# Second block's first columns between the products back, two projections interleaved by pairs of weight pieces, and two steps moved in the attention's queues

## The reference

```python
u2 = modulate(rmsnorm(h, norm_ffn_g[l]), sh2, sc2)
h = h + g2[:, None, :] * hier_moe(u2, ...)          # 16 experts: hid @ w2, summed
return rmsnorm(h, norm_final_g)                     # first block's end
...
xn = rmsnorm_2(h, norm_gain[i]).astype(dt)          # second block's start
proj = xn @ w_in[i]
aq, ak, av, ag, bq, bf, bi, bg, gate_a, gate_b = jnp.split(proj, split_pts, axis=-1)
...
fpre = bf.astype(f32).reshape(b, s, HGRN_HEADS, HGRN_KDIM)
log_f = jax.nn.log_sigmoid(fpre) + jnp.log1p(lb * jnp.exp(jnp.minimum(-fpre, EXP_CLIP)))
kb = (1.0 - lb) * jax.nn.sigmoid(-fpre)
qb = jax.nn.silu(bq.astype(f32)).reshape(b, s, HGRN_HEADS, HGRN_KDIM)
```

## Time and profile before

| | |
|---|---|
| median of 3 runs | 745.0 us (744.92 to 745.93) |
| the profiled execution | 744.99 us, of which span 743.7 us |
| PE busy | 712.0 us (96%), 3766 products |
| DVE busy | 500.4 us (67%) |
| ACT busy | 380.3 us (51%) |
| chain that ended last, by engine | PE 80%, DVE 9%, ACT 4%, DMA 2%, POOL 2% |
| granted TensorE clock, mean | 0.999 |

### The profile page before, as it was taken

The page is one execution under the profiler, slowest core; times in us unless marked ns, Lnnn a source line. Parts: engine busy times, 40 slices in busy tenths (PEclk is TensorE's granted clock), DMA queues, the critical chain, the costliest instruction groups (busy, mean ns, idle before and its releaser), DMA issues.

```text
span 743.7 us, 9899 instructions
## 1 busy us (share of the span) xinstructions
PE 712.0 (96%) x3766; PEld 573.5 (77%) x3766; DVE 500.4 (67%) x738; ACT 380.3 (51%) x549; POOL 90.2 (12%) x71
## 2 busy tenths in 40 slices
PE   3899999999999999999999999989999999999997
PEld 0587666778788877888887777769888877788886
DVE  1364785345579774775668898887998675555854
ACT  1353433556444444654547777747624548644532
POOL 0252385340010000000000000011002500000000
PEclk9999999999999999999999999999999999999999
DMA  9999787757335950666579999955544575536541
GB/s 317 364 291 372 253 323 272 258 171 283 113 116 184 366 175 18 197 221 192 178 242 314 362 349 364 370 203 153 148 132 134 165 224 150 169 117 198 168 141 57
DMA packets 100670, 164.07 MB, mean 221 GB/s; under 512 B 10768, under 2 KB 45293, under 8 KB 100494
## 3 DMA queue, kind: packets, MB, share of 16 engines
q1 hardware_dynamic: 98718, 155.53, 62.9%
q0 software_dynamic: 1904, 7.90, 3.1%
HBM read 162.33 MB, written 1.08 MB: 220 GB/s over the span
## 4 chain that ended last, share of the span: by engine, by line
PE 80%; DVE 9%; ACT 4%; DMA 2%; POOL 2%; SPq 1%; issue 1%; ACTq 0%; DVEq 0%
PE p L574 22%; PE p L576 21%; PE p L575 21%; DVE s_rawr L1841 3%; PE p L643 3%; PE p L632 2%; PE p L1234 2%; ACT s_hi L1395 1%; PE p L702 1%; PE p L678 1%; DMA s_ZC<-in_w_ada_dram 1%; POOL s_BI L492 1%; ACT s_L L1445 1%; DMA s_raw<-in_w_exp_up_dram 1%; PE p L690 1%
## 5 line engine op out<-in xcount | busy, mean ns | idle before, releaser
L1841 DVE TENSOR_TENSOR s_rawr<-s_raw,s_hi 128x1024 fp32r<-128x1024 f32 x223 | 271.8, 1249 | 45.9 <-ACT s_hi L1395 45.3
L1395 ACT ACTIVATE s_hi<-s_raw 128x1024 fp32r<-128x1024 f32 x240 | 245.2, 1054 | 88.0 <-PE p L576 53.7
L574 PE MATMUL p<-s_hi,s_Ah 128*128 128x512 f32 (+1 forms) x464 | 186.5, 402 | 1.7 <-POOL s_rawr L473 1.0
L576 PE MATMUL p<-s_hi,s_Al 128*128 128x512 f32 (+1 forms) x464 | 179.8, 387 | 0.0
L575 PE MATMUL p<-s_rawr,s_Ah 128*128 128x512 f32 (+1 forms) x464 | 179.4, 387 | 0.0
L574 PEld LDWEIGHTS p<-s_hi,s_Ah 128*128 128x128 f32 x464 | 87.3, 188 | 27.0 <-issue 6.9
L576 PEld LDWEIGHTS p<-s_hi,s_Al 128*128 128x128 f32 x464 | 87.2, 188 | 18.4
L575 PEld LDWEIGHTS p<-s_rawr,s_Ah 128*128 128x128 f32 x464 | 87.4, 188 | 15.8 <-issue 0.2
L574 PE MATMUL p<-s_hi,s_Bh 128*128 128x512 f32 x192 | 76.3, 397 | 0.2 <-DVE s_rawr L1841 0.2
L576 PE MATMUL p<-s_hi,s_Bl 128*128 128x512 f32 x192 | 75.0, 391 | 0.0
L575 PE MATMUL p<-s_rawr,s_Bh 128*128 128x512 f32 x192 | 74.9, 390 | 0.0
(11 more groups left out here) (375 smaller groups left out, 857.2 us busy)
## 6 DMA issues: line engine op xcount, KB each, us to landing
s_raw<-in_w_in_dram SPq DMA_DIRECT2D x80, 512.0 KB, 4.0
s_GS<-in_w_ada_dram SPq DMA_DIRECT2D x16, 1024.0 KB, 7.6
s_raw<-in_w_exp_gate_dram SPq DMA_DIRECT2D x64, 256.0 KB, 4.1
s_raw<-in_w_exp_up_dram SPq DMA_DIRECT2D x64, 256.0 KB, 5.4
s_raw<-in_w_exp_down_dram SPq DMA_DIRECT2D x32, 512.0 KB, 5.7
s_raw<-in_w_gate_dram SPq DMA_DIRECT2D x16, 512.0 KB, 5.8
s_raw<-in_w_ret_out_dram SPq DMA_DIRECT2D x8, 512.0 KB, 3.5
s_raw<-in_w_o_dram SPq DMA_DIRECT2D x8, 512.0 KB, 8.4
```

Source lines behind the costliest of these rows:

```text
L574: pe.matmul(o, xh, wh, start=start, stop=False)
L576: return pe.matmul(o, xl, wh, start=False, stop=stop)
L1395: act.activation(T.hi[:, i % NHL, :], T.raw[:, i % NRAW, :], ACT.Copy).then_inc(*S.hi(i))
L1841: dve.tensor_tensor(T.lo[:, i % NRAW, :], T.raw[:, i % NRAW, :], T.hi[:, i % NHL, :].bitcast(F32), ALU.subtract).then_inc(*S.lo_dve(i))
```

## The change

It has five parts. (1) `silu(15)` and `hidden(15)` now stand after the high and low parts of dn14 and before those of dn15. (2) `u3_cols(0)` stands before `rows_back(2, 1)` and `u3_cols(2)` behind it; before, both stood behind it. (3) The pieces of bq and bf are loaded, converted and used in the order bq 0, bq 1, bf 0, bf 1, bq 2, bq 3, bf 2, bf 3, with `u3_cols(4)` in front of bf 0 and `u3_cols(6)` in front of bf 1. VectorE's queue is rewritten to match; ScalarE's stays as it was there, so its conversions now belong to other pieces. (4) The last piece of av is used between the transposes of aq and those of ak. (5) In ScalarE's queue of the attention two conversions move ahead of `exps(0)`, and the copy of the probabilities moves ahead of the silu of ag. No work is added or removed.

```diff
--- before.py
+++ after.py
@@ -88,7 +88,9 @@
             some(f"up{e}", range(4))
         if e:
             some(f"dn{e - 1}", range(2))
-    for name in SECOND:
+    for hs in ((0, 1), (2, 3)):
+        some("bq", hs), some("bf", hs)
+    for name in SECOND[2:]:
         some(name, range(4))
     for n in range(2):
         some(f"ub{n}", range(2)), some(f"ua{n}", range(2))
@@ -1172,6 +1174,11 @@
             q.wait_ge(*S.dve_rows.at("lo", 0, 1))
         down(n, 0, (0, 1), (f"dn{n}", 0, 1))
         down(n, 1, (0, 1), (f"dn{n}", 1, 1))
+
+    def u3_cols(k0):
+        q.wait_ge(*S.dve_moe.at("x3", min(k0 // 2, 2), 1))
+        turn(lambda tt, k: T.X3[:, tt, 128 * k:128 * k + 128], ("u3", k0), S.dve_cols.at("u3", k0))
+
     hidden_cols(15)
     q.wait_ge(*S.dve_rows.at("lo", 1, 1))
     rows_back(0, 0), rows_back(1, 0)
@@ -1180,28 +1187,26 @@
         down(15, 0, (c,), None)
         down(15, 1, (c,), ("dn15", c, 1))
     rows_back(2, 0)
-    rows_back(0, 1), rows_back(1, 1), rows_back(2, 1)
+    rows_back(0, 1), rows_back(1, 1)
+    t_free[0] = t_free[1] = S.dve_moe.at("lo", 15)
+    u3_cols(0)
+    rows_back(2, 1)
+    u3_cols(2)
     m_free[0] = m_free[1] = S.dve_moe.at("gy", 1, 1)
     z_free[0] = z_free[1] = [S.dve_rows.at("lo", 2, 1)]
     z_free[2] = z_free[3] = [S.dve_moe.at("gy", 0, 1)]
-    t_free[0] = t_free[1] = S.dve_moe.at("lo", 15)
-
-
-    def u3_cols(k0):
-        q.wait_ge(*S.dve_moe.at("x3", min(k0 // 2, 2), 1))
-        turn(lambda tt, k: T.X3[:, tt, 128 * k:128 * k + 128], ("u3", k0), S.dve_cols.at("u3", k0))
+
 
     def u3(h):
         return "u3", 2 * h
 
-    u3_cols(0), u3_cols(2)
-    uses("bq", 0, 1, A, u3, turned=True)
+    uses("bq", 0, 2, A, u3, turned=True)
     u3_cols(4)
-    uses("bq", 1, 2, A, u3, turned=True)
+    uses("bf", 0, 1, A, u3, turned=True)
     u3_cols(6)
+    uses("bf", 1, 2, A, u3, turned=True)
     uses("bq", 2, 4, A, u3, turned=True)
     chunk_freed("bq", S.dve_hgrn.at("bq", 0), S.dve_hgrn.at("bq", 1))
-    uses("bf", 0, 2, A, u3, turned=True)
 
     b = turn_bank("norm")
     q.wait_ge(*S.pool_moe.at("r2"))
@@ -1263,13 +1268,13 @@
     uses("bg", 2, 4, A, u3)
     chunk_freed("bg", S.act_moba.at("bg", 0), S.act_moba.at("bg", 1))
     hgrn_out(1)
-    uses("av", 0, 2, A, u3)
-    uses("av", 2, 3, A, u3)
+    uses("av", 0, 3, A, u3)
     for name, z in (("aq", T.ZC[0]), ("ak", T.ZC[1])):
         q.wait_ge(*S.dve_moba.at("norm", name, 1))
         for k0 in (0, 2):
             turn(lambda tt, k: z[:, tt, 128 * k:128 * k + 128], (name, k0), S.dve_moba.at(name, k0))
-    uses("av", 3, 4, A, u3)
+        if name == "aq":
+            uses("av", 3, 4, A, u3)
     chunk_freed("av", S.act_copy.at("av"), S.dve_copy.at("av"))
 
     def moba_logits(tt, g):
@@ -1699,10 +1704,11 @@
         hid_high(n)
         if n == 1:
             third_high()
-        his_to(AT[f"up{n + 2}", 2] if n < 14 else AT["dn15", 1] + 1)
+        his_to(AT[f"up{n + 2}", 2] if n < 14 else AT["dn15", 0])
     silu(15)
+    his_to(AT["dn15", 1] + 1)
     hid_high(15)
-    his_to(AT["bq", 2])
+    his_to(AT["bf", 0])
     rows_out(2, 0), rows_out(2, 1)
 
 
@@ -1782,12 +1788,12 @@
     copy_normed("av", T.AV[:, 0, :], banks("av")[0])
     his_to(AT["sa0", 2])
     cols_scaled("yb", 0, T.Bh, T.g_hg, 4), cols_scaled("yb", 2, T.Bh, T.g_hg, 4)
+    his_to(AT["sa1", 0])
     exps(S.act_moba, S.dve_moba, 0)
-    his(1)
+    his_to(AT["sa1", 2])
+    prob(S.act_moba, S.pe_moba, "moba", 0, 1)
     silu_normed("ag", lambda tt: T.RGS[:, 1, 512 * tt:512 * tt + 512])
-    his(2)
-    prob(S.act_moba, S.pe_moba, "moba", 0, 1)
-    his(2)
+    his_to(AT["sa1", 3])
     gate_second("sa0")
     his(2)
     exps(S.act_moba, S.dve_moba, 1)
@@ -2404,7 +2410,7 @@
         hid_low(n)
         if n == 1:
             third_low()
-        lows_to(AT[f"up{n + 2}", 2] if n < 14 else AT["dn15", 1] + 1)
+        lows_to(AT[f"up{n + 2}", 2] if n < 14 else AT["dn15", 0])
         if n == 2:
             q.wait_ge(*S.final_gain_in.at(0))
             q.wait_ge(*S.dve_ada.at(11))
@@ -2416,8 +2422,9 @@
             q.wait_ge(*S.masks_in.at(0))
             dve.tensor_copy(T.masks[:, :, :], T.G1[:, :].rearrange("p (l t) -> p l t", l=8)).then_inc(*S.dve_moe("masks"))
     hidden(15)
+    lows_to(AT["dn15", 1] + 1)
     hid_low(15)
-    lows_to(AT["bq", 2])
+    lows_to(AT["bf", 0])
     rows_out(2, 0), rows_out(2, 1)
 
 
@@ -2449,17 +2456,19 @@
 
     for j in range(2):
         rows_in(j, 0), rows_in(j, 1)
+    cols_scaled("u3", 0, T.Ah, T.Al, T.g_in2)
     gated(1, 0)
-    cols_scaled("u3", 0, T.Ah, T.Al, T.g_in2)
+    cols_scaled("u3", 2, T.Ah, T.Al, T.g_in2)
     residual(1, 0)
+    lows_to(AT["bf", 1])
     gated(1, 1), residual(1, 1)
-    cols_scaled("u3", 2, T.Ah, T.Al, T.g_in2)
+    lows_to(AT["bq", 2])
+    cols_scaled("u3", 4, T.Ah, T.Al, T.g_in2)
+    gated(0, 0), gated(0, 1)
+    residual(0, 0)
     lows_to(AT["bq", 3])
-    cols_scaled("u3", 4, T.Ah, T.Al, T.g_in2)
-    lows_to(AT["bf", 0])
     cols_scaled("u3", 6, T.Ah, T.Al, T.g_in2)
-    gated(0, 0), gated(0, 1)
-    residual(0, 0), residual(0, 1)
+    residual(0, 1)
     lows_to(AT["bf", 2])
     v = st[:, 488:496].rearrange("p (s n t) -> p s n t", s=2, n=2)
     q.wait_ge(*S.act_moe.at("sq x", 1, 1))
```

## The result

The changed kernel takes 751.42 us (median of 6 runs, 750.18 to 751.57) where the kernel before takes 744.96 us (6 runs, 744.58 to 745.93): ratio 1.0083, 95% interval 1.007 to 1.0096. It is **slower by 6.5 us**; forecast were 5.6 us and 750.6 us, with a range of 747.8 to 752.4. The profiled execution took 751.39 us, of which 750.1 are span.

The account below looks back on a forecast made before the run. The prediction took PE, busy 712.0 of 743.7 us, as the bound, so only its waits count. Hold +6.0, clock +1.2 and attention -1.6 gave +5.6 on 744.99: 750.6 us, range 747.8 to 752.4.

Parts of the forecast that it names:

- The last expert: Transposes of the last hidden row: PE's idle wait of 0.74 us goes, 0.9 us won from start to start.
- Columns between the products back: Before the second block's pieces: bq 0 starts at 497.5 instead of 499.12.
- The hold of bf 0: Bank p_2 waits for gated(0, 1): bf 0 starts at 509.3, PE idle 5.1 us, u3_cols(6) +6.0 us.
- ScalarE's chain to level 0: From u3_cols(6) to the recurrence: nothing caught up, level 0 also +6.0 us, PE waiting 2 us for ScalarE.
- PE's own arrival: At level 0: PE itself there at about 531.4, including 0.8 of waits for low parts of bq 2 and bq 3.
- Rival (b): At level 0 PE's arrival decides, not ScalarE's lateness: +4.1 us, 747.5 to 748.7 us; chance 0.09.
- The clock: Inside bf 0: the granted clock falls to 1.2 GHz after the idle time, +1.2 us; the other end is nothing.
- Rival (a): Around bf 0 the clock holds: 749.4 us; chance 0.27.
- The attention: Parts 4 and 5: waits before ak's transposes and moba_out go, -1.5 to -1.85 us, taken as -1.6.
- Rival (c): The attention gains nothing, its new order delaying something taken as covered: 752.2 us; chance 0.07.
- Rival (d): bf 0 isn't held, gated(0, 1) being done: 744.0 us, or 741.1 if ScalarE's chain doesn't decide; chance 0.08.
- The sum: Whole kernel: +6.0 + 1.2 - 1.6 = +5.6 us on 744.99, giving 750.6 us.

Follow-up runs that it names:

- The fourth experiment: Changed kernel with part 3 (order of the pieces) taken back, parts 1, 2, 4 and 5 left in: 742.29 us, ratio 0.9969.
- The first experiment: Changed kernel with only gated(0, 0) and gated(0, 1) moved ahead of VectorE's low part that waits for ScalarE: 744.74 us, ratio 0.9991.
- the third experiment: Changed kernel with ScalarE's conversion of bf 1 moved ahead of its step on u3_cols(4), u3_cols(6)'s step right behind: 748.63 us, ratio 1.0041.
- the fifth experiment: The first experiment's kernel with ScalarE's squares of x3's first half moved ahead of its step on u3_cols(4): 743.31 us, ratio 0.9973.

## Why the prediction was right, step by step

**The last expert** was to give 0.9 and gave 0.88. **Columns between the products back**: bq 0 was to come 1.6 us earlier and came 1.70 earlier. The fourth experiment shows that these gains are real but were not free to be kept: behind bq 0 the next columns were not ready.

**The hold of bf 0.** The forecast had bf 0 at 509.3; it came at 510.23, which is 509.28 without the 0.95 that was there before the change's first instruction. The wait was to be 5.1 us of idleness and was 5.20, released by L2446 as said, with the links of the chain as said. The step held for a reason a reader can use: it was built from an order (which instruction stands behind which in each queue) and from six durations that the trace of before shows, with no estimate among them. The first experiment confirms it from the other side; the third took two of the links out and won time accordingly.

**ScalarE's chain to level 0.** Nothing was to be caught up, and PE was to wait 2 us: the shift was +7.36 at `u3_cols(6)` and +7.35 at level 0, and PE waited 1.78. PE's own arrival, the start of level 0 less its idle time and less 0.95, was at 532.9, where the forecast gives 532.6 with the clock; the small waits in it were mis-sized, two of 0.26 us before low parts, where I had put 0.8 in all. Rival (b), PE decides, falls by these 1.78 us and by the fifth experiment, in which work taken from ScalarE's queue shortened the wait.

**The clock** was the least sure term: 1.2, with nothing as the other end. It fell, inside bf 0, and cost 1.36 us (4.31 instead of 2.95): 14 products stood 0.21 us apart where I had counted twelve. By the Trainium skill's page "TensorE: Matmul & The Clock Gate", section "Why this matters for your kernels", long idle gaps between bursts of matmuls return the clock to half rate; this trace agrees, and so does the third experiment's. Rival (a), the clock holds, is what the experiment with added transposes made true by force, 749.2 us, where the rival had 749.4.

**The attention** was mis-sized slightly: 1.6, taken near the lower end of 1.5 to 1.85, and it gave 1.88 in the profile and 1.9 in the run by itself. The reason for the lower end was that switching between transposes and products might eat a part; it didn't. The whole distance from start to start was won, as the upper end had it. Rival (c), no gain there, falls by the run with these two parts alone.

**Rival (d)**, in which bf 0 isn't held, didn't happen by itself, and the first experiment made it happen. The rival's 744.0, 1.0 under the kernel before, stood against 744.74 measured, 0.6 under the runs beside it. Its price of 0.65 us for `u3_cols(6)` behind one piece more was too low: 1.4 us, since bf 0 still waited 0.63 for `gated(0, 1)`.

**The sum** was +5.6, and the table gives +5.5 at `moba_out`. That they are so close is partly luck: the clock cost 0.16 more than forecast and the attention gave 0.28 more, and the two offset each other. The measured +6.5 (+6.4 in the profiled pair) contains, in that pair, the 0.95 us from the first 40 us. The first three experiments point the same way. Each one's median plus the distance by which its level 0 comes earlier than in the changed kernel gives an estimate of what the changed kernel takes: 744.74 + 5.93 = 750.7, 749.23 + 1.32 = 750.6, 748.63 + 1.88 = 750.5. That is 5.1 to 5.3 us above the 745.37 of the kernel before beside them. The six runs of the changed kernel have a median some 0.8 above these estimates, with one of them at 750.18. That their first 40 us happened to be slow ones is the reading that fits; since only one of the six has a trace, it isn't shown.
